# First block's pooled up, up and output projections as three split products

## The chip, the cores and the metric

The kernel runs on one core of one Trainium2 chip. The metric is the device time in microseconds (us) of one execution. A core has five engines with queues of their own: PE (TensorE, matrix products), DVE (VectorE), ACT (ScalarE), POOL (GpSimd) and SP (SyncE, which here issues the loads). Semaphores order their work. SBUF is the on-chip memory, PSUM the banks into which PE writes.

## What is computed

Two transformer-like blocks, one after the other, on 256 tokens of width 1024, all in float32. The first block, where the change lies:

```python
ada = c @ w_ada[layer] + b_ada[layer]
shift1, scale1, gate1, shift2, scale2, gate2 = split(ada, 6)
h = rms_norm(x, g_norm1) * (1.0 + scale1) + shift1
z = h @ w_in
zq, zk, zv, ziq, zik, ziw, zp, zg = split(z, cuts)
...
y_attn = dsa_attention(q, k, zv, iq, ik, ziw) @ w_up_attn[layer]   # 512 -> 1024
y_pool = pool_mixer(zp, w_pool_grp, s_pool) @ w_up_pool[layer]     # 512 -> 1024
g_attn, g_pool = split(sigmoid(zg), 2)
mixed = (g_attn * y_attn + g_pool * y_pool) @ w_out[layer]         # 1024 -> 1024
x = x + gate1 * mixed
h2 = rms_norm(x, g_norm2) * (1.0 + scale2) + shift2
x = x + gate2 * peer_ffn(h2, w_peer_q, peer_subkeys, peer_u, peer_v)
```

`dsa_attention` has 8 heads of 64 and lets each token see 64 chosen positions; `peer_ffn` is dense here over all 128 x 128 experts. The second block (recurrent branch, sparse attention, feed-forward) comes after it and isn't touched beyond the naming of two buffers.

## The kernel before

**The stream of weights.** All weight matrices lie in one stream of quarters of 128 x 1024 numbers (512 KB). `ORDER` (from `plan`) is the order of the blocks: ada0 to ada3, in0 to in6, up_pool, ada9, ada4, up_attn, out0, out1, pq0, pq1, the expert matrices u and v, then the second block. A block is four quarters. Blocks in `PAIRED` alternate with an ada block, quarter by quarter: in1 with ada6, in6 with ada7, up_pool with ada8, out0 with ada5, out1 with ada10, pq1 with ada11. SP loads quarter b into slot b % 4 of `ring`, strictly in the order of the stream; it waits until `left[b % 4]` says that quarter b - 4 has left its slot. A quarter that isn't free holds up all loads behind it.

**Two kinds of quarters.** A quarter marked in `SPLIT` is taken apart: ACT rounds it into `high` (`round_quarter`), POOL subtracts to give `low` (`lower_quarter`) and thereby frees the ring slot; PE makes a product as three (`product`, high x high, high x low, low x high), and its end (`multiplied`) frees the slot of `high` and `low`. The moving or stationary input is kept as a pair too (`hTh`, `hTl`). Any other quarter is read straight from the ring: PE's product is then one full-precision matmul (the profile shows two records of it), and the ring slot is free when PE is done. The ada quarters are read by DVE, two `scalar_tensor_tensor` of 128x512 each (the first one a `tensor_scalar`), which add up `c @ w_ada` by rows; PE sums over the partitions later (`ada`). Before the change `in`, `pq`, `u`, `v` and the second block's weights are split; up_pool, up_attn, out0 and out1 are not. `high` and `low` have four slots, chosen by b % 4 like the ring's, so in a paired block only two of them are used.

**Order by hand.** Each engine runs its own program from top to bottom. ACT's roundings stand where the program calls `ahead(name, q, n)`: it rounds every split quarter up to n quarters behind quarter q of that block; `wait_product` calls it with n = 3 and then waits for PE. A rounding that has to wait for its load or its slot holds up all that ACT has to do behind it.

**The stretch of the change,** in PE's order: `z1(6)` (in6), up_pool (`token_major`, 4 quarters of 4 products 128x512, 2 token tiles by 2 halves), the attention of 8 units (`attention("a1")`: logits, transposes, values, in a software pipeline with ACT's Exp and copies and DVE's maxima, normalizations and copies; DVE also adds up ada9 and ada4, one quarter a unit), up_attn (its last two quarters output by output, `bank_done`), the transposes of the gated mix M1 (`transposes("m1")`), the sums of ada6 to ada9, out0, the first half of out1 (`out1(0, 1)`), the sums of ada4 and ada5 which give gate1, the second half of out1 (`out1(2, 3)`, both quarters waited for before its first product), the second norm and pq0.
DVE, behind the attention: the pooled branch times its gate (L1648), some constants of the second block (L1650 to L1662, 22 short steps), the gating of the four outputs of up_attn (L1671, L1672), half of the copies of M1's transposes, ada5, ada10, then x1 from out0 and out1 (L1694, L1695).
ACT, behind the attention: the two halves of its output (L1155), half of M1's copies (`keep_turned`, L1030), the copies of the gate (L1162), the squares of x1 (L998).

## Time and profile before

| | us |
|---|---|
| median of 3 runs | 1657.17 |
| lowest, highest | 1652.24, 1659.6 |
| the profiled execution | 1656.26 |
| its span in the trace | 1654.4 |
| PE busy in the span | 1556.4 |
| DVE, ACT, POOL busy | 1101.6, 840.4, 1103.9 |
| mean granted clock of PE | 0.977 |

Times in the trace count from the start of the span. The clock is a share of 2.4 GHz and has two levels, 1.0 and 0.5; a mean between them tells how much of the stretch ran at each. The profile's busy times of PE are those of its matmuls; weight loads (PEld) run beside them.

### The profile page before, as it was taken

The numbers are of one execution on the slowest core, as the hardware profiler recorded it, in microseconds if no ns is written. First come the engines' busy times: TensorE is split into PE (matmuls) and PEld (weight loads), VectorE is DVE, ScalarE is ACT, GpSimd is POOL, SyncE is SP. The second block draws the span as 40 slices with busy tenths as digits, with TensorE's granted clock in tenths as the row PEclk, the third lists the DMA queues.
The fourth block names the chain that finished last, engine by engine and source line by source line (L and its number), as shares of the span: only waits on it lengthen the run. The fifth ranks groups of instructions, "written<-read, shape, count | busy, mean of one in ns | idle before, by whom it ended". The sixth has DMA issues, their size and how long they took to land. (4 is left out here: it accounts for less than half of the span.)

```text
span 1654.4 us, 27016 instructions
## 1 busy us (share of the span) xinstructions
PE 1556.4 (94%) x9679; PEld 1359.3 (82%) x9679; DVE 1101.6 (67%) x1666; ACT 840.4 (51%) x1437; POOL 1103.9 (67%) x453
## 2 busy tenths in 40 slices
PE   2898898999999999999999999999999988999999
PEld 2685537999999999988888888888888756799987
DVE  5563645999937777768888888761756275368850
ACT  1454215555566666655445554547764354554443
POOL 0771006889986666658888888855985621688896
PEclk9999789999999999999999999999999889999999
DMA  7665355455454444435555555545554510455554
GB/s 278 207 230 203 127 181 201 165 178 178 153 190 141 140 141 141 141 127 190 190 194 193 196 190 191 198 141 176 192 192 140 166 52 26 153 179 182 187 179 140
DMA packets 77397, 280.07 MB, mean 169 GB/s; under 512 B 8577, under 2 KB 9089, under 8 KB 77186
## 3 DMA queue, kind: packets, MB, share of 16 engines
q1 hardware_dynamic: 76592, 276.68, 49.3%
q10 hardware_dynamic: 722, 2.27, 0.4%
q8 instruction: 55, 0.90, 0.2%
q14 instruction: 28, 0.23, 0.1%
HBM read 277.86 MB, written 1.05 MB: 169 GB/s over the span
## 5 line engine op out<-in xcount | busy, mean ns | idle before, releaser
L2071 POOL TENSOR_TENSOR low<-ring,high 128x1024 fp32r<-128x1024 f32 x449 | 1103.7, 2470 | 539.9 <-ACT high L977 539.3
L977 ACT ACTIVATE high<-ring 128x1024 fp32r<-128x1024 f32 x449 | 472.8, 1058 | 438.1 <-PE PS L346 381.7
L344 PE MATMUL PS<-hTh,high 128*128 128x256 f32 (+1 forms) x1648 | 472.7, 287 | 9.7 <-POOL low L2071 7.5
L346 PE MATMUL PS<-hTh,low 128*128 128x256 f32 (+1 forms) x1648 | 467.9, 284 | 0.0
L345 PE MATMUL PS<-hTl,high 128*128 128x256 f32 (+1 forms) x1648 | 467.8, 284 | 0.0
L344 PE MATMUL PS<-high,hTh 128*128 128x512 f32 x940 | 370.6, 394 | 14.4 <-POOL low L2071 5.9
L345 PE MATMUL PS<-low,hTh 128*128 128x512 f32 x940 | 367.9, 391 | 0.0
L346 PE MATMUL PS<-high,hTl 128*128 128x512 f32 x940 | 367.8, 391 | 0.0
L1801 DVE TENSOR_TENSOR hTl<-region,hTh 128x256 fp32r<-128x256 f32 x128 | 289.2, 2261 | 57.9 <-ACT hTh L1231 57.9
L344 PEld LDWEIGHTS PS<-hTh,high 128*128 128x128 f32 (+1 forms) x1648 | 316.3, 192 | 13.0 <-POOL low L2071 9.2
L345 PEld LDWEIGHTS PS<-hTl,high 128*128 128x128 f32 (+1 forms) x1648 | 316.2, 192 | 0.0
L346 PEld LDWEIGHTS PS<-hTh,low 128*128 128x128 f32 (+1 forms) x1648 | 315.8, 192 | 0.0
L344 PEld LDWEIGHTS PS<-high,hTh 128*128 128x128 f32 x940 | 177.9, 189 | 54.4 <-issue 10.4
L346 PEld LDWEIGHTS PS<-high,hTl 128*128 128x128 f32 x940 | 177.7, 189 | 37.3
L345 PEld LDWEIGHTS PS<-low,hTh 128*128 128x128 f32 x940 | 178.1, 189 | 36.4
L1204 ACT ACTIVATE onehot<-gate,gate_rest 128x128 fp32r<-128x128 f32 x256 | 82.1, 391 | 66.8 <-DVE gate L1763 66.8
L1560 DVE SCALAR_TENSOR_TENSOR region<-ring,cols,region 128x512 f32<-128x512 f32 x84 | 75.3, 897 | 49.6 <-DMA ring<-in_stream 46.5
L1774 DVE TENSOR_TENSOR region<-region,PS 128x256 f32<-128x256 f32 (+31 forms) x64 | 35.3, 551 | 61.6 <-PE PS L771 61.6
L342 PE MATMUL PS<-ring,region 128*128 128x512 f32 x128 | 63.5, 654 | 3.0 <-ACT region L1083 1.2
L771 PE MATMUL PS<-onehot 128*128 128x128 f32 x256 | 60.7, 276 | 0.0
L342 PEld LDWEIGHTS PS<-ring,region 128*128 128x128 f32 x128 | 26.1, 210 | 38.8 <-issue 31.5
L770 PE MATMUL PS<-onehot 128*128 128x128 f32 x256 | 57.1, 261 | 0.7 <-ACT onehot L1204 0.7
(283 smaller groups left out, 1535.1 us busy)
## 6 DMA issues: line engine op xcount, KB each, us to landing
ring<-in_stream SPq DMA_DIRECT2D x523, 512.0 KB, 3.3
X<-in_x SPq DMA_DIRECT2D x1, 1024.0 KB, 5.1
region<-in_band ACTq DMA_DIRECT2D x1, 1024.0 KB
result<-X SPq DMA_DIRECT2D x4, 256.0 KB, 2.0
region<-in_skeys ACTq DMA_DIRECT2D x1, 512.0 KB
region<-in_consts ACTq DMA_DIRECT2D x1, 352.0 KB, 3.4
region<-in_wpool ACTq DMA_DIRECT2D x1, 256.0 KB
cols<-in_cols SPq DMA_DIRECT2D x1, 208.0 KB, 5.1
```

The source lines that it names most:

```text
L342: return pe.matmul(out_, stat, mov, start=start, stop=stop, **kw)
L344: pe.matmul(out_, sh, mh, start=start, stop=False, **kw)
L345: pe.matmul(out_, sh, ml, start=False, stop=False, **kw)
L346: return pe.matmul(out_, sl, mh, start=False, stop=stop, **kw)
L770: pe.matmul(dst, rows[:, j, :], high_[:, j, :], start=True, stop=False)
L771: last = pe.matmul(dst, rows[:, j, :], rest[:, j, :], start=False, stop=True)
L977: act.activation(high[:, b % RING, :], ring[:, b % RING, :], ACT.Copy).then_inc(rounded[b % RING], 1)
L1204: ins = act.activation(fours(onehot[:, 2, g % 2, :])[:, j, :], fours(second[:, g % 2, :])[:, j, :], ACT.Copy, scale=gate_rest[:, 4 * g + j ...
L1560: ins = dve.scalar_tensor_tensor(ada_acc(j), w[:, c, :], col("cT", 2 * q + c), ada_acc(j), ALU.mult, ALU.add)
L1774: dve.tensor_tensor(v[:, 0:n, :], v[:, 0:n, :], placed[:, 0:n, :], ALU.mult)
L1801: dve.tensor_tensor(lo, src, hi.bitcast(F32), ALU.subtract).then_inc(sem("weights_split"), 1)
L2071: pool.tensor_tensor(low[:, b % RING, :], ring[:, b % RING, :], high[:, b % RING, :].bitcast(F32), ALU.subtract).then_inc(left[b % RING], 1)
```

## The change

The quarters of up_pool, up_attn, out0 and out1 are split as well. The slot in `high` and `low` (and of `rounded` and `multiplied`) is no longer b % 4 but the number of split quarters before b, modulo 4 (`part`); the ring and `left` stay at b % 4. The pooled input becomes a pair (`pool_parts`: ACT rounds, POOL subtracts, in POOL's order just before up_pool's first quarter). The attention's output goes as a pair into the first half of hT (DVE subtracts, behind the attention and ahead of L1648), and the transposed mix as a pair into hT (`mixed_high`, `mixed_low`) in place of `keep_turned`. ACT's roundings of the new quarters are placed: up_pool's first with `z1(6)`, its second behind the copies of in6, its last two behind the two sigmoids; up_attn's, one each, at the end of the last four steps of the attention; out0's first two behind the attention's output, its third behind `mixed_high`, its fourth and out1's first two behind the copy of the ada sums, out1's last two behind the two copies of gate1. The diff, cut:

```diff
--- before.py
+++ after.py
@@ -121,13 +121,21 @@
-SPLIT = [NAME_AT[b].rstrip("0123456789") in ("in", "pq", "u", "v", "rx", "ry", "z", "ro", "ao", "oo", "fg", "fv",
+SPLIT = [NAME_AT[b].rstrip("0123456789") in ("in", "up_pool", "up_attn", "out", "pq", "u", "v", "rx", "ry", "z", "ro", "ao", "oo", "fg", "fv",
                                                 "dn") for b in range(N_QUARTERS)]
...
+SPLIT_NO = [0] + np.cumsum(SPLIT).tolist()
+
+
+def part(b):
+
+    return SPLIT_NO[b] % RING
+
+
 def nth_split(b):
-    return sum(SPLIT[i] for i in range(b % RING, b + 1, RING))
+    return SPLIT_NO[b] // RING + 1
@@ -217,10 +225,10 @@
         poolT = take(4, S)
-        OT1 = take(4, S)
+        pool_parts = Pair(onehot[:, w, :, :].rearrange("p a n -> p (a n)") for w in (1, 2))
         late_acc = take(ADA_B - 4, NB)
         y_pool = XN1
-        M1, MT1 = N1, NT1
+        M1 = N1
         LB1 = band.rearrange("p t g s -> p (t g s)")[:, 0:3 * 2 * S].rearrange("p (u e k) -> p u e k", u=3, e=2)
@@ -322,7 +330,7 @@
             if SPLIT[b]:
-                eng.wait_ge(multiplied[b % RING], nth_split(b))
+                eng.wait_ge(multiplied[part(b)], nth_split(b))
             else:
...
@@ -347,13 +355,14 @@
+        MIXED1, MIXED2 = 0, KC // 2
         TURNS = ("n1", "m1", "n2", "n3", "q2", "c2", "k2", "pz", "m2", "n4")
...
-        KEPT = {"m1": KC, "q2": KC, "k2": KC, "c2": 2 * KC, "pz": KC}
+        KEPT = {"q2": KC, "k2": KC, "c2": 2 * KC, "pz": KC}
@@ -404,7 +413,10 @@
             b = quarter_no(name, q)
-            ins.then_inc((multiplied if SPLIT[b] else left)[b % RING], 1)
+            if SPLIT[b]:
+                ins.then_inc(multiplied[part(b)], 1)
+            else:
+                ins.then_inc(left[b % RING], 1)
@@ -521,15 +533,15 @@
             def token_major(name, src, bank, per=2, rows=P, first=True, last=True, inner=NB, c0=0, norm=None,
-                            bank_done=None, quarters=range(QUARTERS), mixed=False):
+                            bank_done=None, quarters=range(QUARTERS), mixed=None):
...
                         pe.wait_ge(sem("norm_split"), nth_norm(norm, KC // 2, (per * h + per + 1) // 2))
-                    if mixed:
-                        pe.wait_ge(sem("mixed_split"), h + 1)
+                    if mixed is not None:
+                        pe.wait_ge(sem("mixed_split"), mixed + h + 1)
                     w = slot(name, h, inner)
@@ -691,23 +703,23 @@
             pe.wait_ge(sem("z_kept"), 2 * Z1B)
-            token_major("up_pool", poolT, lambda t, o: 4 + (2 + 2 * t + o) % 4, per=1, inner=D)
+            pe.wait_ge(sem("pool_split"), 1)
+            token_major("up_pool", pool_parts.rearrange_all(S), lambda t, o: 4 + (2 + 2 * t + o) % 4, per=1, inner=D)
             pe.wait_ge(sem("y_pool_kept"), 4)
...
-            pe.wait_ge(sem("attn1_kept"), 2)
-            token_major("up_attn", OT1, lambda t, o: 4 + 2 * t + o, per=1, inner=D, bank_done="up_done")
+            pe.wait_ge(sem("attn1_split"), 2)
+            token_major("up_attn", hT, lambda t, o: 4 + 2 * t + o, per=1, inner=D, bank_done="up_done")
             transposes("m1", M1, "m1_ready", 4, first_half=3)
...
                 ada(j)
-            pe.wait_ge(sem("turned_kept"), kept_by("m1", KC))
             def out1(*quarters, done=None):
-                token_major("out1", MT1, lambda t, o: 5 + 2 * t, quarters=quarters, bank_done=done)
-
-            token_major("out0", MT1, lambda t, o: 4 + 2 * t)
+                token_major("out1", hT, lambda t, o: 5 + 2 * t, quarters=quarters, bank_done=done)
+
+            token_major("out0", hT, lambda t, o: 4 + 2 * t, mixed=MIXED1)
             pe.wait_ge(sem("ada_kept"), 2)
...
@@ -936,7 +948,7 @@
             for half in range(2):
-                token_major(f"oo{half}", hT, lambda t, o, half=half: 4 + 2 * t + half, mixed=(half == 0),
+                token_major(f"oo{half}", hT, lambda t, o, half=half: 4 + 2 * t + half, mixed=None if half else MIXED2,
                             bank_done="oo_done" if half else None)
@@ -973,9 +985,9 @@
                 if nth_split(b) > 1:
-                    act.wait_ge(multiplied[b % RING], nth_split(b) - 1 + r)
-                act.activation(high[:, b % RING, :], ring[:, b % RING, :],
-                               ACT.Copy).then_inc(rounded[b % RING], 1)
+                    act.wait_ge(multiplied[part(b)], nth_split(b) - 1 + r)
+                act.activation(high[:, part(b), :], ring[:, b % RING, :],
+                               ACT.Copy).then_inc(rounded[part(b)], 1)
@@ -1018,6 +1030,13 @@
+            def mixed_high(tag):
+
+                for c in range(0, KC, 2):
+                    act.wait_ge(sem("turned"), turned_by(tag, c // 2 + 1))
+                    act.activation(hTh[:, c:c + 2, :], PS[:, c // 2, :].rearrange("p (c s) -> p c s", c=2),
+                                   ACT.Copy).then_inc(sem("mixed_rounded"), 1)
+
             def keep_turned(tag, dst, scale=None, shift=None):
@@ -1060,6 +1079,8 @@
                         kept(u - 2)
+                    if tag == "a1" and u >= n - 2:
+                        ahead("up_attn", u - (n - 2), 0)
                     if tag == "a2" and u == n // 2 + 2:
@@ -1137,12 +1158,16 @@
                                scale=col("gain1", 0)).then_inc(sem("qk1_kept"), 1)
+            act.wait_ge(sem("pool_kept"), 4)
+            act.activation(tuple(pool_parts)[0], poolT.rearrange("p g s -> p (g s)"),
+                           ACT.Copy).then_inc(sem("pool_rounded"), 1)
             z1(6)
+            ahead("up_pool", 1, 0)
             act.wait_ge(sem("z_kept"), 2 * Z1B)
...
                                ACT.Sigmoid).then_inc(sem("sig1"), 1)
-            wait_used(act, "up_pool")
+            wait_product("up_pool")
             for t in range(T):
@@ -1152,15 +1177,19 @@
                 act.wait_ge(sem("a1_values"), (t + 1) * H1 // 2)
-                act.activation(OT1[:, :, t * P:(t + 1) * P], PS[:, 6 + t, :].rearrange("p (c q) -> p c q", c=4),
-                               ACT.Copy).then_inc(sem("attn1_kept"), 1)
-            keep_turned("m1", MT1)
+                act.activation(hTh[:, 0:4, t * P:(t + 1) * P], PS[:, 6 + t, :].rearrange("p (c q) -> p c q", c=4),
+                               ACT.Copy).then_inc(sem("attn1_rounded"), 1)
+            ahead("out0", 1, 0)
+            mixed_high("m1")
+            ahead("out0", 2, 0)
             act.wait_ge(sem("ada_summed"), 8)
             act.activation(adaT[:, 24:40], PS[:, 7, 24:40], ACT.Copy).then_inc(sem("ada_copied"), 1)
+            ahead("out1", 1, 0)
             for i in range(2):
...
                                ACT.Copy).then_inc(sem("gate1_kept"), 1)
+            ahead("out1", 3, 0)
             sumsq("n2", XN1, "x1_ready")
...
@@ -1378,10 +1407,7 @@
                     ahead(f"ao{half}", q)
-            for c in range(0, KC, 2):
-                act.wait_ge(sem("turned"), turned_by("m2", c // 2 + 1))
-                act.activation(hTh[:, c:c + 2, :], PS[:, c // 2, :].rearrange("p (c s) -> p c s", c=2),
-                               ACT.Copy).then_inc(sem("mixed_rounded"), 1)
+            mixed_high("m2")
             for half in range(2):
@@ -1459,6 +1485,13 @@
                     ins.then_inc(sem("norm_split"), 1)
+
+            def mixed_low(done):
+
+                for c in range(0, KC, 2):
+                    dve.wait_ge(sem("mixed_rounded"), done + c // 2 + 1)
+                    dve.tensor_tensor(hTl[:, c:c + 2, :], PS[:, c // 2, :].rearrange("p (c s) -> p c s", c=2),
+                                      hTh[:, c:c + 2, :].bitcast(F32), ALU.subtract).then_inc(sem("mixed_split"), 1)
@@ -1641,6 +1674,11 @@
             attention("a1")
+            for t in range(T):
+                qs = slice(t * P, (t + 1) * P)
+                dve.wait_ge(sem("attn1_rounded"), t + 1)
+                dve.tensor_tensor(hTl[:, 0:4, qs], PS[:, 6 + t, :].rearrange("p (c q) -> p c q", c=4),
+                                  hTh[:, 0:4, qs].bitcast(F32), ALU.subtract).then_inc(sem("attn1_split"), 1)
@@ -1671,7 +1709,7 @@
                                       ALU.add).then_inc(sem("m1_ready"), 1)
-            keep_turned("m1", MT1)
+            mixed_low(MIXED1)
@@ -2004,10 +2042,7 @@
                                       ALU.add).then_inc(sem("m2_ready"), 1)
-            for c in range(0, KC, 2):
-                dve.wait_ge(sem("mixed_rounded"), c // 2 + 1)
-                dve.tensor_tensor(hTl[:, c:c + 2, :], PS[:, c // 2, :].rearrange("p (c s) -> p c s", c=2),
-                                  hTh[:, c:c + 2, :].bitcast(F32), ALU.subtract).then_inc(sem("mixed_split"), 1)
+            mixed_low(MIXED2)
             for half in range(2):
@@ -2067,12 +2102,17 @@
-                pool.wait_ge(rounded[b % RING], nth_split(b) + r)
-                pool.tensor_tensor(low[:, b % RING, :], ring[:, b % RING, :], high[:, b % RING, :].bitcast(F32),
+                pool.wait_ge(rounded[part(b)], nth_split(b) + r)
+                pool.tensor_tensor(low[:, part(b), :], ring[:, b % RING, :], high[:, part(b), :].bitcast(F32),
                                    ALU.subtract).then_inc(left[b % RING], 1)
...
             for b in range(START["in0"], first):
+                if b == quarter_no("up_pool", 0):
+                    high_, low_ = tuple(pool_parts)
+                    pool.wait_ge(sem("pool_rounded"), 1)
+                    pool.tensor_tensor(low_, poolT.rearrange("p g s -> p (g s)"), high_.bitcast(F32),
+                                       ALU.subtract).then_inc(sem("pool_split"), 1)
                 if SPLIT[b]:
```

## Rows read from the trace of the kernel before

**Rows 1.** The page, section 1: busy us, share of the span, instructions by engine.

```profile
PE 1556.4 (94%) x9679; PEld 1359.3 (82%) x9679; DVE 1101.6 (67%) x1666; ACT 840.4 (51%) x1437; POOL 1103.9 (67%) x453
```

**Rows 2.** Windows by stage; the header names the columns.

```profile
core 0: us, PE busy (x) PEld busy (x) DVE busy (x) ACT busy (x) POOL busy (x), PEclk, DMA share, GB/s
...
139.80:157.40 17.60, 14.27 (x32) 5.88 (x32) 4.60 (x7) 8.16 (x10) 0.00 (x0) 1.00 0.59 217
157.40:184.40 27.00, 22.24 (x120) 14.26 (x120) 24.04 (x50) 11.88 (x44) 0.00 (x0) 0.64 0.55 187
184.40:200.40 16.00, 15.96 (x33) 6.85 (x34) 8.29 (x29) 0.00 (x0) 0.00 (x0) 0.87 0.20 66
...
207.10:231.90 24.80, 23.76 (x48) 9.77 (x49) 8.84 (x14) 0.18 (x1) 0.00 (x0) 0.89 0.58 209
231.90:236.50 4.60, 4.60 (x11) 1.28 (x9) 1.50 (x2) 0.60 (x1) 0.00 (x0) 1.00 0.64 232
236.50:245.30 8.80, 8.80 (x17) 3.59 (x16) 5.49 (x8) 4.25 (x9) 0.00 (x0) 0.81 0.08 17
245.30:257.00 11.70, 5.99 (x30) 5.38 (x30) 9.68 (x18) 6.14 (x11) 2.35 (x1) 0.71 0.61 216
```

**Rows 3.** Timeline of weight loads: split products (in6), then full-precision ones (up_pool).

```profile
128.62 0.19 PEld L344 LDWEIGHTS PS<-high,hTh 128*128 128x128 f32 x1
...
129.30 0.19 PEld L344 LDWEIGHTS PS<-high,hTh 128*128 128x128 f32 x1
...
142.35 0.19 PEld L342 LDWEIGHTS PS<-ring,region 128*128 128x128 f32 x1 [0.24 <-issue]
142.78 0.19 PEld L342 LDWEIGHTS PS<-ring,region 128*128 128x128 f32 x1 [0.24 <-issue]
```

**Rows 4.** Groups by form, 120 to 262 us (count, busy, mean ns); DMA issues (landing us).

```profile
L1560 DVE SCALAR_TENSOR_TENSOR region<-ring,cols,region 128x512 f32<-128x512 f32 x41 | 30.8, 751 | 33.2 <-DMA ring<-in_stream 32.2
L2071 POOL TENSOR_TENSOR low<-ring,high 128x1024 fp32r<-128x1024 f32 x6 | 14.2, 2377 | 129.8 <-ACT high L977 129.8
...
L977 ACT ACTIVATE high<-ring 128x1024 fp32r<-128x1024 f32 x8 | 8.1, 1048 | 6.7 <-PE PS L346 6.7
...
ring<-in_stream SPq DMA_DIRECT2D x47, 512.0 KB, 3.3
```

**Rows 5.** Timeline (start us, us, engine), POOL and DVE where their work overlaps.

```profile
63.02 2.77 DVE L1560 SCALAR_TENSOR_TENSOR region<-ring,cols,region 128x512 f32<-128x512 f32 x1 [1.28 <-DMA ring<-in_stream]
...
65.42 2.62 POOL L2071 TENSOR_TENSOR low<-ring,high 128x1024 fp32r<-128x1024 f32 x1 [0.18 <-ACT high L977]
...
250.71 2.35 POOL L2071 TENSOR_TENSOR low<-ring,high 128x1024 fp32r<-128x1024 f32 x1 [113.99 <-ACT high L977]
...
251.63 1.97 DVE L1456 TENSOR_TENSOR hTl<-region,hTh 128x512 fp32r<-128x512 f32 x1
```

**Rows 6.** Timeline, end of the attention: ACT's copies, DVE's normalization and ada4.

```profile
174.66 0.38 ACT L1055 ACTIVATE region<-PS 128x256 f32<-128x256 f32 x1
...
176.99 0.69 DVE L1508 TENSOR_TENSOR region<-region 128x512 f32<-128x512 f32 x1
...
177.84 0.38 ACT L1055 ACTIVATE region<-PS 128x256 f32<-128x256 f32 x1
...
177.94 1.53 DVE L1560 SCALAR_TENSOR_TENSOR region<-ring,cols,region 128x512 f32<-128x512 f32 x2
```

**Rows 7.** Timeline, DVE behind the attention: pooled branch, chain's end, last gating.

```profile
182.21 2.47 DVE L1648 TENSOR_TENSOR region<-region 128x1024 f32<-128x1024 f32 x2
...
189.10 0.17 DVE L1662 TENSOR_SCALAR sp<-sp 126x11 f32<-126x11 f32 x1
...
201.31 0.69 DVE L1672 TENSOR_TENSOR region<-PS,region 128x512 f32<-128x512 f32 x1
```

**Rows 8.** Timeline: second gate copy, DVE on out1's last output, the norm's transposes.

```profile
236.59 0.60 ACT L1162 ACTIVATE region<-PS 128x512 f32<-128x512 f32 x1 [1.51 <-PE PS L509]
...
245.34 0.70 DVE L1694 TENSOR_TENSOR PS<-PS,region 128x512 f32<-128x512 f32 x1 [2.01 <-PE PS L342]
...
249.12 2.74 PE L483 MATMUL PS<-ident,region 128*128 128x128 f32 x16 [3.82 <-ACT region L1006]
```

More of the change, by code:

```diff
@@ L744, in peer_u @@
                                    hT[:, c, :], start=(c == 0), stop=(c == KC - 1))
-                last.then_inc(multiplied[b % RING], 1)
+                last.then_inc(multiplied[part(b)], 1)
             pe.wait_ge(sem("scores_kept"), 8)
@@ L790, in peer_v @@
                                        skip_group_check=True)
-                last.then_inc(multiplied[b % RING], 1)
+                last.then_inc(multiplied[part(b)], 1)
             pe.wait_ge(sem("ada_kept"), 4)
@@ L816, in _ @@
                         if t and half:
-                            last.then_inc(multiplied[b % RING], 1)
+                            last.then_inc(multiplied[part(b)], 1)
                     if not (t and half):
```

6 lines of the change are left out of this document (3 added, 3 removed).

## The prediction

> **What bounds the kernel now.** I read the page first. PE is busy for 94% of the span, DVE and POOL for 67% each [rows 1], and from the expert products on the matmuls of one stage follow those of the next without a gap. So whatever the first block's projections shift, everything behind them is shifted by as much. I then cut the stretch of the change into its stages [rows 2]: the pooled up projection (139.8 to 157.4 us), the attention (157.4 to 184.4), the attention's up projection (184.4 to 200.4), `out0` with the first half of `out1` (207.1 to 231.9), the two gate sums (231.9 to 236.5), the second half of `out1` (236.5 to 245.3), and the second norm. PE is busy for nearly all of each projection stage: they are bound by the full-precision products. In none of them does POOL do anything. That last column matters most below. The mean granted clock of a stage tells how long PE ran at the lower of its two levels (1.2 GHz against 2.4): 0.87 over 16.0 us is 2 x 0.13 x 16.0 = 4.2 us at half, 0.89 over 24.8 us is 5.5 us, 0.81 over 8.8 us is 3.3 us.
>
> **What is removed.** A full-precision product shows as two records. Their weight loads stand 0.43 us apart at 2.4 GHz [rows 3], so one costs 0.86 us. A split product shows as three; equal loads stand 0.68 us apart for 512 columns at 2.4 GHz [rows 3]. 0.43 us is the time of two passes of 512 columns at 2.4 GHz; at 1.2 GHz a pass takes 0.43, so the products cost 1.71 and 1.28. The change makes 4 quarters x 4 = 16 products in each of up_pool, up_attn, out0 and out1, 64 in all: 64 x 0.174 = 11.1 us of PE at full clock, and 0.43 instead of 0.17 each at half clock.
>
> The Trainium skill ("FP8 and Floating Point Precision", TensorE Precision Notes) says that true FP32 makes four passes through the array; three of four would save 25%, 13.7 us over the 64 products. The pitches give 20%, and the sum goes by them.
>
> **What is added.** Each of the 16 quarters now gets a rounding on ACT (1.05 us) and a subtraction on POOL (2.38 us), one after the other [rows 4]. The ring slot is given back when POOL is done, 3.4 us after the rounding starts; before, it was given back after PE's four products, also 3.4 us. The load behind it still needs 3.3 us to land [rows 4]. New too: one rounding and one subtraction for the pooled input (`pool_parts`), DVE subtractions for the attention output and the mixed input (0.7 us each for 128x512), and larger copies on ACT in place of `keep_turned`.
>
> **The price that isn't in the instruction counts** is DVE against POOL. When POOL starts a subtraction at 250.71 and DVE, at 251.63, a `tensor_tensor` whose inputs both lie in SBUF, DVE's ends at 253.60, 0.54 us after POOL's (253.06). At 63.02 a DVE `scalar_tensor_tensor` beside another subtraction takes 2.77 us; POOL's next, asked for at 65.42 while that one finishes (65.79), takes 2.62 itself [rows 5]. The same DVE instruction takes 0.75 us where POOL is idle [rows 4]. So the two exclude each other for whole instructions, first come first served: a DVE instruction with two SBUF inputs that meets a subtraction waits up to 2.4 us.
>
> The Trainium skill ("SBUF — State Buffer", Who interferes with whom) states this: a DVE instruction with two SBUF inputs contends with a GpSimd instruction that reads SBUF, and the later one blocks fully. By that rule the trace agrees; the rule speaks against this change, which puts POOL work where POOL has now been idle for 114 us.
>
> **The sum, stage by stage,** on the profiled execution's own clock. I replay each queue in its program order with the durations above.
>
> *in6 and up_pool: 0.* The rotation over split quarters lets in6's third quarter be rounded without waiting for its first one's products: some 0.5 us. up_pool's quarters 2 and 3 are rounded only behind the sigmoids, so PE waits some 3 us (146.2 to 149.5) before quarter 2. Sixteen products at 0.68 with that wait end near 155.3, where the 16 full-precision ones end now. Everything in the stage (two ACT roundings, `pool_parts`, DVE's ada8) is then paid for.
>
> *Attention: +7.2.* The four up_attn quarters are rounded in ACT's last four steps. The first is rounded when ACT is free at 175.04 [rows 6], its subtraction runs 176.1 to 178.5. DVE's unit-6 normalization, now at 176.99 [rows 6], waits and ends at 179.0. The next rounding runs from 178.2 (after the copy of 177.84 [rows 6]), so the second subtraction holds 179.3 to 181.7; DVE's last two accumulations for ada4, now 177.94 to 179.47 [rows 6], meet it and the third one (182.2 to 184.5) and end at 185.05 instead. Up_attn's last quarter is loaded behind them: issued 185.1, landed 188.4, rounded 189.5. In the meantime unit 7's normalization runs at 185.4, 5.8 us late, and its values end at 188.6. ACT copies the two output halves behind that rounding (190.7), DVE subtracts the second (191.6). PE starts up_attn at 191.6 instead of 184.44. Of this 5.6 us are waits for POOL; without them it would be +1.5.
>
> *up_attn: +0.1.* With 4.3 us at half clock first, 3.4 products are made, the other 12.6 take 8.6 us; the first output would be ready at 200.5. But DVE's gating of the pooled branch and the decay chain, now 182.21 to 189.3 [rows 7], begin at 191.6 and meet the subtractions for out0's first two quarters (197.6 to 202.7): they end at 203.4. The four outputs take DVE 4 x 1.46 us, to 209.3, now 202.0 [rows 7]. The transposes and ada sums behind (PE, 5.1 us from 202.0 to out0's start at 207.1) are unchanged, and hide the split of the mixed input. out0 starts at 214.4 instead of 207.1: +7.3.
>
> *out0, out1: -0.5.* out0's fourth quarter is behind a quarter of ada5 in SP's queue, whose slot DVE frees at 216.4; it lands at 220.3, is rounded, and lowered at 224.4. By then PE, after 5.5 us at half clock, is at 225.2: no wait. out1's first quarters are lowered at 227.2 and 231.2, PE is done with them at 233.9. 24 products took 19.5 us, now 24.8. The gate sums end at 238.4 (4.5 us), ACT copies the second gate (0.6 us [rows 8]), and only then rounds out1's last two quarters: 239.0, two roundings, then 2 x 2.38 us on POOL. PE needs both and starts at 244.9: **6.5 us idle**, the new wait. Now the same chain costs nothing, as the quarters lie in the ring. Eight products then take 5.5 us, or 7.2 if the first 3.4 us run at half clock. I take 7.2: the pause of 3.8 us before the norm's transposes (245.3 to 249.12 [rows 8]) is followed today by a clock of 0.71 in that stage [rows 2]. The last x1 is at 253.6; now at 245.34 + 1.42 = 246.8 [rows 8]. Together +6.8.
>
> *After that: 0.* pq0's first rounding and the norm are chains of ACT and DVE as before. pq1's quarters rotate better, but the last one's rounding stands behind a copy that waits for PE either way.
>
> The sum is 1656.26 + 6.8 = **1663 us**. The profiled execution lies 0.9 us below the median of 1657.17; the three runs spread over 7 us. Against the median this is +0.35%. About 0.5%, 8.3 us, is what a measurement here can tell from no change, so this is *no change, on the slower side*.
>
> Not shown by the trace, with bounds. A DVE instruction on the decay chain is 126x11: whether it too is excluded is between 0 and 4.5 us (two subtractions met); its nearest rows are the 128x512 ones, so I take it as excluded. Two-input normalization in the attention: 0 to 5.6 us, taken in full for the same reason. ACT's rounding between two Exp: 0 to 1.3 us for a table load; the copies there today bring none, so 0. The pause of up_pool: 0 to 1.7 us for clock, taken as 0, as 3.3 us lies under the 3.8 after which it fell; it may go either way.
>
> **Rivals.**
> A, *the exclusion doesn't reach these instructions.* For it: they are smaller than those in rows 5, and POOL runs few. Against: rows 5, both forms. The waits of 5.6 in the attention and of 3 us on the decay chain vanish; up_attn starts at 186.0, out0 at 206.0, the pause before out1's last quarters stays, x1 ends at 243 to 244.6. That is -2.2 to -3.9: 1653. Chance 0.13.
> B, *slower by over 0.5%: one more stretch at half clock.* PE's pauses grow (3.3 us in up_pool, a longer attention tail, 6.5 us before out1). Every further 3.4 us at half clock costs 1.7 us, and the time passes 1665.5, 0.5% over the median, with 2.4 us on top of my sum: from two such stretches on (3.4), or from one with one more subtraction met by DVE (1.7 + 1.9). Both stretches and the subtraction give 1663.1 + 5.3 = 1668. For it: the attention stage is already at 0.64 [rows 2]. Against: pauses also let loads and roundings run ahead. Chance 0.33.
> C, *faster by over 0.5%.* The 11.1 us of PE reach the end: neither the exclusion nor the 6.5 us pause is there, because ACT and POOL are ahead wherever they are needed. A's -3 and the pause's -6.5: 1647. Against it is ACT's program order, in which the two roundings stand behind the gate copies. Chance 0.07.
> D, *the rotation does nothing or more than the 0.5 us of in6.* In the stages with all quarters split the buffers are the same as now. The paired stretches in1 and pq1 wait for loads or for an ACT order that stays. It would be 1662 or 1664, inside the forecast.
>
> **How the numbers follow.** Forecast 0.47 (1659 to 1665.4; D lies in it), A 0.13, B 0.33, C 0.07. Within 0.5%: 0.47 + 0.13 = 0.60; slower 0.33; faster 0.07. For 8 in 10 the range takes in A and most of B: 1652 to 1670, leaving out C and B's end.
>
> **What the profile after would show.** PE products of the four projections as three records 0.68 apart. DVE normalizations of units 6 and 7, and the last ada4 accumulations, at 1.9 to 2.8 us. up_attn starting some 7 us later against in6's end; PE idle for about 6 us, released by POOL, between the gate sums and out1's end. If POOL's subtractions run beside DVE instructions of 0.7 us, the attention term is wrong; if PE has no wait there, the out1 term is. Wrong altogether if up_pool's quarters are late by more than 3 us, or if DVE picks up the attention later than the replay.

## The result, and the profile after

The changed kernel takes 1664.49 us (median of 11 runs, 1662.13 to 1668.36), the kernel before in the same comparison 1653.80 us (11 runs, 1646.96 to 1660.14): ratio 1.007, interval 1.0051 to 1.0089. It is slower by 10.7 us. The predicted time of 1663 us is 1.5 us off and the range holds it; but the predicted *difference*, 0.35%, is half of the measured one, and 0.7% is past the 0.5% up to which the forecast spoke of no change. By the ratio this is rival B, given 0.33; by the time it isn't, as B begins at 1665.5 us and 1664.49 lies within the forecast's 1659 to 1665.4. The two disagree because the three runs of before that were shown (median 1657.17) lie 3.4 us over all eleven. The profiled execution took 1662.13 us, its span 1660.3.

Section 1 of the page of the changed kernel answers [rows 1]:

```profile
PE 1546.7 (93%) x9743; PEld 1375.3 (83%) x9743; DVE 1125.1 (68%) x1668; ACT 858.0 (52%) x1454; POOL 1144.4 (69%) x470
```

PE is busy for 9.7 us less, near the 11.1 us of the split products, and the kernel is longer all the same. The windows of the changed kernel, by stage, answer [rows 2]: in6 from its ninth TensorE record on (1.9 us behind its first) with up_pool; attention; up_attn; transposes and ada sums; out0 with half of out1; gate sums; second half of out1 up to the norm's transposes. Then the same stages of the *kernel before in a second execution*, profiled later (e12 below):

```profile
core 0: us, PE busy (x) PEld busy (x) DVE busy (x) ACT busy (x) POOL busy (x), PEclk, DMA share, GB/s
127.80:157.60 29.80, 22.97 (x89) 17.14 (x87) 12.84 (x10) 14.61 (x17) 16.14 (x7) 0.94 0.59 212
157.60:191.40 33.80, 22.07 (x121) 14.10 (x121) 28.76 (x51) 15.51 (x48) 9.36 (x4) 0.63 0.47 160
191.40:205.20 13.80, 13.69 (x48) 10.77 (x48) 12.86 (x31) 2.12 (x2) 5.33 (x3) 0.80 0.29 103
205.20:211.50 6.30, 5.99 (x48) 5.75 (x49) 3.89 (x6) 3.11 (x5) 2.10 (x1) 0.92 0.00 0
211.50:232.10 20.60, 19.79 (x73) 15.43 (x74) 13.19 (x15) 3.37 (x4) 7.51 (x4) 0.86 0.72 254
232.10:242.70 10.60, 4.18 (x9) 1.07 (x7) 5.32 (x8) 5.79 (x10) 4.65 (x2) 0.77 0.26 93
242.70:254.70 12.00, 8.18 (x24) 6.28 (x24) 3.84 (x8) 2.48 (x7) 0.00 (x0) 0.78 0.36 140
```

```profile
128.20:156.30 28.10, 23.87 (x73) 12.98 (x71) 6.93 (x11) 10.27 (x11) 4.76 (x2) 1.00 0.54 195
156.30:183.20 26.90, 21.41 (x121) 13.63 (x121) 24.10 (x50) 11.78 (x44) 0.00 (x0) 0.68 0.56 187
183.20:197.00 13.80, 13.80 (x32) 6.00 (x33) 8.24 (x29) 0.00 (x0) 0.00 (x0) 1.00 0.23 76
197.00:203.10 6.10, 5.47 (x49) 5.24 (x49) 2.81 (x6) 1.21 (x4) 0.00 (x0) 1.00 0.48 173
203.10:227.80 24.70, 23.12 (x50) 9.56 (x50) 8.85 (x14) 0.18 (x1) 0.00 (x0) 0.93 0.57 199
227.80:231.90 4.10, 4.10 (x9) 1.07 (x7) 1.43 (x2) 0.60 (x1) 0.00 (x0) 1.00 0.82 288
231.90:242.90 11.00, 7.19 (x18) 3.00 (x17) 7.99 (x15) 6.08 (x14) 0.00 (x0) 1.00 0.46 164
```

Three things stand in these lines. POOL's column is no longer empty behind the attention's start. PE is idle for 11.7 us of the attention (before 5.5) and for 6.4 us of the gate sums' window (before 0). And the granted clock is under 1 in all seven stages of the changed kernel, in two of the second execution of before.

The table lays out every kernel of this study in that way. A column is the time from the first TensorE record of one part (for in6 the ninth) to that of the next in the profiled execution, in brackets the us of it at 1.2 GHz, 2 x (1 - granted clock) x length.

| kernel | in6, up_pool | attention | up_attn | sums | out0, half of out1 | gate sums | rest of out1 | all |
|---|---|---|---|---|---|---|---|---|
| before | 28.1 (0) | 27.0 (20) | 15.9 (4.3) | 6.8 (1.4) | 25.2 (5.5) | 4.1 (0) | 12.6 (3.4) | 119.8 |
| e12, before again | 28.2 (0) | 26.8 (17) | 13.8 (0) | 6.1 (0) | 24.7 (3.4) | 4.1 (0) | 11.0 (0) | 114.7 |
| after | 29.8 (3.4) | 33.8 (25) | 13.9 (5.5) | 6.3 (1.0) | 20.6 (5.8) | 10.6 (4.9) | 12.0 (5.3) | 127.0 |
| e11, after again | 28.4 (0) | 33.8 (26) | 15.9 (4.4) | 5.9 (0.3) | 20.7 (3.1) | 10.6 (4.4) | 12.3 (5.8) | 127.7 |
| e1, lowering late | 29.9 (3.4) | 28.2 (17) | 18.7 (5.1) | 10.2 (10) | 20.9 (5.3) | 10.6 (5.7) | 11.6 (4.8) | 130.1 |
| e2, rounding early | 29.9 (3.4) | 33.9 (25) | 14.1 (5.9) | 6.1 (0.7) | 20.8 (6.1) | 5.8 (0) | 11.1 (4.3) | 121.7 |
| e3, both | 30.1 (3.4) | 28.3 (20) | 18.9 (5.2) | 10.2 (10) | 20.5 (5.9) | 5.3 (0) | 11.1 (3.7) | 124.3 |
| e4, rotation alone | 26.8 (0) | 26.9 (17) | 13.8 (0) | 6.4 (0.6) | 24.1 (2.9) | 4.1 (0) | 11.0 (0) | 113.0 |
| e5, POOL alone | 28.6 (0) | 32.2 (21) | 13.8 (0) | 6.1 (0) | 23.9 (3.4) | 4.1 (0) | 11.0 (1.2) | 119.7 |
| e6, POOL writes | 28.1 (0) | 26.7 (16) | 16.2 (4.8) | 6.5 (0.8) | 25.6 (6.0) | 4.1 (0) | 12.7 (3.4) | 119.9 |
| e7, up_attn whole | 30.1 (3.4) | 26.9 (18) | 16.6 (5.5) | 6.2 (0.2) | 25.6 (10) | 4.1 (0) | 9.6 (0) | 118.9 |
| e8, out0 and out1 | 26.9 (0) | 26.9 (18) | 16.6 (5.6) | 6.2 (0.1) | 25.5 (10) | 4.4 (0) | 9.7 (0) | 116.1 |
| e9, out1 alone | 27.0 (0) | 26.9 (17) | 13.8 (0) | 6.1 (0) | 26.9 (6.8) | 5.1 (0) | 9.5 (0.5) | 115.3 |
| e10, no rotation | 30.5 (3.4) | 33.8 (26) | 13.7 (4.4) | 7.0 (2.6) | 31.2 (15) | 10.6 (3.4) | 11.1 (4.3) | 137.9 |

Read it by columns: a stage's length is a matter of PE's passes, its pauses and its time at 1.2 GHz, and the last differs between two executions of one kernel (up_attn of before: 4.3 us at half once, none in the other, 2.1 us apart). "Half clock" below is the 1.2 GHz of the brackets.

### The profile page after: what moved, and what is told of

It is laid out like the page before. It is cut to its first block and busy times, and to the rows that moved or that the text cites. A ratio compares the mean times of both kernels' runs of the same rounds, so it can differ in the third digit from the quotient of the medians.

```text
span 1660.3 us, 27119 instructions
## 1 busy us (share of the span) xinstructions
PE 1546.7 (93%) x9743; PEld 1375.3 (83%) x9743; DVE 1125.1 (68%) x1668; ACT 858.0 (52%) x1454; POOL 1144.4 (69%) x470
## 5 line engine op out<-in xcount | busy, mean ns | idle before, releaser
L2106 POOL TENSOR_TENSOR low<-ring,high 128x1024 fp32r<-128x1024 f32 x465 | 1142.2, 2469 | 505.3 <-ACT high L989 504.7
L989 ACT ACTIVATE high<-ring 128x1024 fp32r<-128x1024 f32 x465 | 489.5, 1057 | 452.4 <-PE PS L354 376.3
L352 PE MATMUL PS<-high,hTh 128*128 128x512 f32 x988 | 392.9, 398 | 21.9 <-POOL low L2106 11.3
L353 PE MATMUL PS<-low,hTh 128*128 128x512 f32 x988 | 389.9, 395 | 0.0
L354 PE MATMUL PS<-high,hTl 128*128 128x512 f32 x988 | 389.5, 394 | 0.0
L352 PEld LDWEIGHTS PS<-hTh,high 128*128 128x128 f32 (+1 forms) x1648 | 316.2, 192 | 12.7 <-POOL low L2106 8.5
L352 PEld LDWEIGHTS PS<-high,hTh 128*128 128x128 f32 x988 | 189.1, 191 | 65.0 <-issue 19.2
L354 PEld LDWEIGHTS PS<-high,hTl 128*128 128x128 f32 x988 | 188.7, 191 | 40.3
L1593 DVE SCALAR_TENSOR_TENSOR region<-ring,cols,region 128x512 f32<-128x512 f32 x84 | 89.0, 1059 | 28.9 <-DMA ring<-in_stream 25.9
L495 PE MATMUL PS<-ident,region 128*128 128x128 f32 x160 | 27.6, 343 | 31.3 <-ACT region L1018 23.5
L495 PEld LDWEIGHTS PS<-ident,region 128*128 128x128 f32 x160 | 24.6, 179 | 34.6 <-issue 15.5
```

Source lines behind the costliest of these rows:

```text
L352: pe.matmul(out_, sh, mh, start=start, stop=False, **kw)
L353: pe.matmul(out_, sh, ml, start=False, stop=False, **kw)
L354: return pe.matmul(out_, sl, mh, start=False, stop=stop, **kw)
L495: last = pe.transpose(PS[:, c // 2, (c % 2) * S + t * P:(c % 2) * S + (t + 1) * P], src[:, t, c * P:(c + 1) * P], ident[:, :])
L989: act.activation(high[:, part(b), :], ring[:, b % RING, :], ACT.Copy).then_inc(rounded[part(b)], 1)
L1593: ins = dve.scalar_tensor_tensor(ada_acc(j), w[:, c, :], col("cT", 2 * q + c), ada_acc(j), ALU.mult, ALU.add)
```

## The experiments

**The attention (e5, e6).** Does POOL's subtraction make the attention late, or ACT's new work and the late load? Both kernels are the one before with the same ACT copies, and three POOL instructions behind them:

```diff
 ACT, in attention("a1")
+                    if tag == "a1" and n - 2 <= u < n + 1:
+                        act.activation(high[:, (0, 1, 3)[u - (n - 2)], :], high[:, 2, :].bitcast(F32),
+                                       ACT.Copy).then_inc(sem("extra_rounded"), 1)
 ACT, ahead of out1's further roundings
+            act.wait_ge(sem("extra_done"), 3)
 POOL, ahead of up_attn's quarters
+                    for k in range(3):
+                        pool.wait_ge(sem("extra_rounded"), k + 1)
+                        pool.tensor_tensor(low[:, (0, 1, 3)[k], :], low[:, 2, :].bitcast(F32),
+                                           high[:, (0, 1, 3)[k], :].bitcast(F32), ALU.subtract).then_inc(sem("extra_done"), 1)
+                    pool.wait_ge(sem("extra_done"), 3)
 POOL in e6, in place of the subtraction
+                        pool.memset(low[:, (0, 1, 3)[k], :].bitcast(F32), 0.0).then_inc(sem("extra_done"), 1)
```

> The kernel before, with three ACT copies and three POOL subtractions of 128x1024 put into the end of the attention, where the changed kernel has those of up_attn's first three quarters; their results are used by nobody. All projections stay full precision. Theory (DVE instructions with two SBUF inputs wait for POOL's subtraction): unit 6's normalization takes 1.9 to 2.1 us instead of 0.69, ada4's last two accumulations 4.5 to 5.6 us instead of 1.53, and the attention's up projection starts 5 to 6 us later than in the kernel before (some 190 instead of 184.4 us, counted from the same start of the attention). Rival (the attention's tail is late because of ACT's roundings between the Exp, or the late load): DVE's instructions keep 0.69 and 1.53 us and the projection starts at most 1.5 us later.

> As the run with POOL's subtractions alone, but POOL fills the same three 128x1024 tiles with zeros (it writes SBUF and reads nothing). If what excludes DVE is that POOL reads SBUF, DVE's normalization and accumulations keep 0.69 and 1.53 us and up_attn starts within 1.5 us of the kernel before. If any POOL instruction on SBUF excludes them, they stretch as beside the subtractions, by the length of the fill, and up_attn starts later by 2 us or more.

Timelines (start us, us, engine, line, operation) of e5, then of e6: DVE's normalization (L1512; of unit 6 in e5, of unit 7 in e6) and ada4's last accumulations (L1564) beside POOL:

```profile
174.97 2.43 POOL L2083 TENSOR_TENSOR low<-low,high 128x1024 fp32r<-128x1024 f32 x1 [39.09 <-ACT high L1064]
175.90 2.05 DVE L1512 TENSOR_TENSOR region<-region 128x512 f32<-128x512 f32 x1
178.15 5.10 POOL L2083 TENSOR_TENSOR low<-low,high 128x1024 fp32r<-128x1024 f32 x2 [0.75 <-ACT high L1064]
178.21 5.59 DVE L1564 SCALAR_TENSOR_TENSOR region<-ring,cols,region 128x512 f32<-128x512 f32 x2
```

```profile
177.39 1.53 DVE L1564 SCALAR_TENSOR_TENSOR region<-ring,cols,region 128x512 f32<-128x512 f32 x2
178.68 0.95 POOL L2083 MEMSET low<- 128x1024 f32 x1 [2.23 <-ACT high L1064]
179.03 0.69 DVE L1512 TENSOR_TENSOR region<-region 128x512 f32<-128x512 f32 x1
```

The two take 2.05 and 5.59 us beside the subtractions, 0.69 and 1.53 beside the fill (unit 6's normalization in e6, at 176.45, begins as the first fill ends and tells nothing). The fills are shorter, 0.95 us against 2.43, and lie beside DVE's instructions for 0.6 and 0.2 us only; but neither DVE nor POOL waits there. The attention takes 32.16 us in e5 and 26.74 in e6, no more than in the kernel before. The two kernels share ACT's copies, so the 5.4 us are POOL's alone, and come where it reads SBUF. Their whole times (1653.36 and 1660.83 us, one execution each) go the other way: e6 has 15 us at half clock between the attention and the norm, e5 has 5, and one execution can't size 5 us of 1650. What DVE does beside the two kinds of POOL's work is the rule of the Trainium skill ("SBUF — State Buffer", Who interferes with whom): a GpSimd instruction that only writes does not contend with a DVE instruction of two SBUF inputs. The trace agrees.

**Moving the wait away (e1).** POOL begins up_attn's subtractions only behind the last normalization:

```diff
+                if b == quarter_no("up_attn", 0):
+                    pool.wait_ge(sem("a1_norm"), H1)
```

> The kernel after with one more wait: POOL begins up_attn's four subtractions only when DVE has made the attention's last normalization. ACT's roundings stay. My theory (POOL and DVE exclude each other, 5.6 us of the attention's tail is DVE waiting): unit 6's normalization is back at 0.69 us from 2.04, the last two accumulations of ada4 at 1.5 from 5.59, up_attn starts 5 to 6 us earlier against the attention's start; DVE's pooled branch now meets subtractions (up to 2.4 us more), up_attn's last quarters come late by 2 to 3 us; net 2 to 4 us faster than the kernel after. Rival (the rounding on ACT in the chain is the price, POOL isn't): no more than 1 us comes back.

1666.13 us (6 runs), ratio 1.0071 (1.0052 to 1.009): nothing gained. The attention did get shorter by 5.6 us, but the subtractions now meet the next DVE work:

```profile
182.88 7.99 POOL L2106 TENSOR_TENSOR low<-ring,high 128x1024 fp32r<-128x1024 f32 x3
185.99 5.96 DVE L1686 TENSOR_TENSOR region<-region 128x1024 f32<-128x1024 f32 x2
192.24 4.83 POOL L2106 TENSOR_TENSOR low<-ring,high 128x1024 fp32r<-128x1024 f32 x2 [1.38 <-ACT high L989]
192.45 2.23 DVE L1690 TENSOR_TENSOR sp<-sp 126x11 f32<-126x11 f32 x1
194.71 2.39 DVE L1691 TENSOR_TENSOR sp<-sp 126x11 f32<-126x11 f32 x1
200.72 0.69 DVE L1709 TENSOR_TENSOR PS<-PS,region 128x512 f32<-128x512 f32 x1
```

The pooled branch takes 5.96 us (2.47 where POOL is idle [rows 7]), two links of the decay chain 2.23 and 2.39 (0.17 each). The gating starts at 200.72; in the changed kernel's first execution at 201.05. DVE's chain from the attention to the gating is what up_attn's outputs wait for, and it pays for the subtractions wherever they are put. The transposes behind then ran at half clock throughout (10.2 us).

**The pause before out1's last quarters (e2, e3).**

```diff
-            ahead("out1", 1, 0)
+            ahead("out1", 3, 0)
             for i in range(2):
...
-            ahead("out1", 3, 0)
```

> The kernel after with out1's last two roundings moved ahead of the two copies of gate1 on ACT. Theory (the 6.46 us in which PE is idle before out1's last quarters are ACT's order, not the loads): the quarters are loaded by 229.4 and 232.7, rounded by 233.8, lowered by 236.2, the idle time falls to under 1 us, and the products that ran at half clock behind it run at full, 1.7 us more: 6 to 8 us faster than the kernel after. Rival (the loads or POOL set it): 0 to 2 us.

> Both edits. Theory: the two costs are in series, so the gains add: 8 to 12 us faster than the kernel after, that is from 2 us slower to 4 us faster than the kernel before by its profiled execution's sum. Rival (the extra time is the granted clock, whatever the pauses): the gains don't add, and it stays over 0.5% slower than before.

e2: 1661.19 us (12 runs), ratio 1.0037 (1.0021 to 1.0053), 0.33% or 5.5 us under the changed kernel's, though the two intervals just touch; the stretch of the table is 5.3 us shorter. The wait of PE, in the changed kernel and in e2:

```profile
242.74 0.77 PE L352 MATMUL PS<-high,hTh 128*128 128x512 f32 x1 [6.46 <-POOL low L2106]
```

```profile
240.49 0.77 PE L352 MATMUL PS<-high,hTh 128*128 128x512 f32 x1 [1.67 <-POOL low L2105]
```

4.8 us of pause are gone and about 5.5 gained: this wait was on the path in full, and about half of the loss. e3, with e1's edit on top: 1662.22, 1.004 (1.0019 to 1.0062), the same as e2; e1's edit is worth nothing here either.

**Which projections pay (e7, e8, e9).** e7 is e2 with up_attn in full precision; e8 leaves up_pool in full precision too; e9 splits out1 alone, with e2's order of roundings, and makes the pair of the mixed input later, on ACT and DVE from the copy that out0 reads. Where a projection isn't split, the work for its pair of inputs goes with it. The line of SPLIT:

```diff
 e7: ... in ("in", "up_pool", "out", "pq", ...)
 e8: ... in ("in", "out", "pq", ...)
 e9: ... in ("in", "pq", ...) or NAME_AT[b] == "out1"
```

> The changed kernel with out1's quarters rounded before the gate copies, and with up_attn left in full precision, so that POOL has nothing to do in the attention, nor beside the decay chain. Theory (the loss is POOL against DVE around the attention): the attention takes 27 us as in the kernel before, up_attn starts at its time, out0 begins where it did (some 50 us after the attention's start) and the two output projections save up to 5.5 us of PE. Median 4 to 6 us below the kernel before (ratio 0.997), so 10 us below the run with the early roundings alone. Rival (three-record products lose by themselves, through PE's clock or the loads, wherever they are): ratio 1.001 to 1.004, above the kernel before still.

> As the run with up_attn whole, but up_pool in full precision too: only the two output projections are split. Theory (up_pool's gain of 2.7 us on PE is paid for by the pause before its third quarter and by ACT's two more roundings): within 1.5 us of that run. If up_pool's split is worth its PE time, this one is 2 to 3 us slower; if its pause costs more, through the clock too, 2 us or more faster.

> The kernel before with the rotation over split quarters and out1 alone split (mixed input rounded and lowered from the kept copy, out1's quarters rounded before the gate copies); up_pool, up_attn and out0 in full precision. Theory (a split gains only where its quarters lie loaded early enough to hide 3.4 us of rounding and lowering): the 16 products of out1 save 2.8 us, the second half of out1 takes 9.6 us as in the two runs with it split early instead of 11.0, and the ratio to the kernel before is 0.997 (rotation alone 0.9985, and 2.8 us less). Rival (the new subtractions delay ada5 and ada10 on DVE and through them out1's loads): PE waits 2 us or more for POOL ahead of out1's first quarters, and the ratio is 0.999 or above.

| | products split | PE us saved at full clock (x 0.174) | median, us | ratio to before |
|---|---|---|---|---|
| e7 | 48 | 8.4 | 1657.68 | 1.0029 (1.0008 to 1.0051) |
| e8 | 32 | 5.6 | 1654.94 | 1.0002 (0.9981 to 1.0022) |
| e9 | 16 | 2.8 | 1655.90 | 1.0013 (0.9998 to 1.0028) |

Here my theory fell, as far as it went for the whole loss. The attention is back at 26.9 us in all three, and the second half of out1 takes 9.5 to 9.7 us instead of 11.0 (8 x 0.174 = 1.4, as priced); yet none of the three is measurably faster than the kernel before. e9 shows why at its plainest, around out1's first quarter:

```profile
217.63 1.06 ACT L991 ACTIVATE high<-ring 128x1024 fp32r<-128x1024 f32 x1 [13.43 <-DMA ring<-in_stream]
218.77 2.63 POOL L2101 TENSOR_TENSOR low<-ring,high 128x1024 fp32r<-128x1024 f32 x1 [85.39 <-ACT high L991]
221.54 0.47 PE L353 MATMUL PS<-high,hTh 128*128 128x512 f32 x1 [3.88 <-POOL low L2101]
```

The quarter lands at 217.63, which is 62.7 us behind the attention's start, as in e4 below (62.8): the load isn't late. PE, free at 217.66, could take it at once in full precision; it waits 3.88 us for the rounding and the subtraction: more than 16 products save. In e8 PE waits for out0's fourth quarter in the same stage:

```profile
207.35 2.37 POOL L2094 TENSOR_TENSOR low<-ring,high 128x1024 fp32r<-128x1024 f32 x1 [1.69 <-ACT high L989]
207.38 2.38 DVE L1704 TENSOR_TENSOR adaT<-adaT,cols 128x16 f32<-128x16 f32 x1 [1.16 <-ACT adaT L1180]
...
216.37 1.06 ACT L989 ACTIVATE high<-ring 128x1024 fp32r<-128x1024 f32 x1 [9.02 <-DMA ring<-in_stream]
217.50 2.34 POOL L2094 TENSOR_TENSOR low<-ring,high 128x1024 fp32r<-128x1024 f32 x1 [7.78 <-ACT high L989]
...
219.89 0.80 PE L353 MATMUL PS<-high,hTh 128*128 128x512 f32 x1 [4.36 <-POOL low L2094]
```

A DVE instruction on 128x16 elements meets a subtraction and takes 2.38 us; ada5 and the ring slots that it frees are later by that. The quarter lands at 216.37, 0.8 us after PE is free, and 3.5 us of rounding and lowering come on top. From the stage's first product to the landing it is 10.8 us, no longer than in full precision (11.9 in e4, where PE doesn't wait for it): PE with split products is there sooner, and the quarter has to be ready 3.5 us before that. PE pauses for 4.36 us, and 10 us of the stage run at half clock against 3.4 and 5.5 in the two executions of before.

e7 has the same pause, and it shows where the time went that the attention gave back:

```profile
224.07 0.80 PE L353 MATMUL PS<-high,hTh 128*128 128x512 f32 x1 [4.74 <-POOL low L2099]
```

out0's fourth quarter lands 61.4 us behind the attention's start in e2 and 60.8 in e7, but PE begins out0 54.1 us behind it in e2 and 49.6 in e7. The stage takes 20.8 us there and 25.6 here. POOL's delay in the attention had hidden the wait for this quarter; without it the wait is PE's.

e7 against e8 is the price of up_pool's split: 30.1 against 26.9 us in the first column (28.4 in e11, which has no half clock there), 0.27% by the medians' ratios, though the intervals overlap. The pause before its third quarter (3.08 us at 150.22 in e7, 2.87 in the changed kernel) is followed by 3.4 us at half clock in six of the seven executions that have this split, and in none of the seven without it is there any in that column.

**The rotation (e4, e10).** e4 is the kernel before with `part(b)` and `nth_split(b)` as in the change and nothing else; e10 is the changed kernel with these two lines back:

```diff
-    return SPLIT_NO[b] % RING
+    return b % RING
-    return SPLIT_NO[b] // RING + 1
+    return sum(SPLIT[i] for i in range(b % RING, b + 1, RING))
```

> The kernel before with nothing but the rotation of the split buffers over split quarters. Theory: in6 ends 0.5 us earlier, all else as before: -0.5 us, not to be told from before (ratio 0.998 to 1.002). Rival (the rotation is worth something in the paired blocks in1, in6 and pq1): 2 us or more faster.

> The changed kernel with the split buffers numbered by the ring slot, as in the kernel before, so that a split projection paired with a full precision one has two of the four buffers. Theory (the loss has nothing to do with the buffers, and the rotation gave the 1.3 us by which the stretch from in5 to the attention got shorter with the rotation alone): 1 to 3 us slower than the changed kernel, ratio to the kernel before 1.008 to 1.009. Rival (the rotation costs something in the changed kernel, as roundings run further ahead and POOL meets DVE more often): faster than the changed kernel, ratio 1.005 or less.

e4: 1652.26 us (12 runs), ratio 0.9985 (0.9967 to 1.0003); in6 and up_pool take 26.8 instead of 28.1 us. e10: 1676.11 (4 runs), 1.0133 (1.011 to 1.0156). In the changed kernel the rotation is worth 0.63%, 10.4 us; without it the change would have cost 22. e10's timeline of ACT, POOL and PE in the out0 stage:

```profile
218.94 1.06 ACT L989 ACTIVATE high<-ring 128x1024 fp32r<-128x1024 f32 x1 [8.94 <-PE PS L354]
219.91 0.16 ACT L1186 ACTIVATE adaT<-PS 128x16 f32<-128x16 f32 x1
...
229.16 1.06 ACT L989 ACTIVATE high<-ring 128x1024 fp32r<-128x1024 f32 x1 [9.09 <-DMA ring<-in_stream]
230.29 2.34 POOL L2106 TENSOR_TENSOR low<-ring,high 128x1024 fp32r<-128x1024 f32 x1 [7.84 <-ACT high L989]
...
232.69 0.79 PE L352 MATMUL PS<-high,hTh 128*128 128x512 f32 x1 [7.16 <-POOL low L2106]
```

With two buffers for out0's quarters, the rounding of the third waits for PE's products with the first (8.94 us). Behind it in ACT's program stands the copy of `adaT`: 219.91 instead of 211.70 in the changed kernel. DVE's ada5 starts behind that copy, the slots come free late, the fourth quarter lands at 229.16 instead of 218.76 (the stage itself began 2.4 us later), and PE pauses for 7.16 us, with 15 us of the stage at half clock.

**Second executions (e11, e12)**, both kernels unchanged:

> The changed kernel once more, for a second profiled execution. If the stage times of the first are the kernel's own, the attention takes 33 to 34.5 us, up_pool with in5 and in6 29.5 to 30.5 us and the gate sums with the pause 10 to 11 us again; if they are chance of PE's clock, one of them moves by 2 us or more.

> The kernel before once more, for a second profiled execution. If its first one was a slow draw of PE's clock in up_attn (4.3 us at half), this execution has less at half clock in up_attn and out1, and a time of 1645 to 1653 us; if not, it has the same stretches and 1654 to 1658 us.

e11 (1662.75 us) repeats the attention and the gate sums to 0.1 us; in6 and up_pool are 1.4 us shorter, with no time at half clock, and up_attn is 2.0 longer. That isn't the clock (4.4 us at half against 5.5), but DVE's decay chain, which here meets both subtractions for out0's first quarters; PE waits for the gating behind it:

```profile
196.65 4.84 POOL L2106 TENSOR_TENSOR low<-ring,high 128x1024 fp32r<-128x1024 f32 x2 [6.01 <-ACT high L989]
196.78 2.29 DVE L1697 TENSOR_SCALAR sp<-sp 126x11 f32<-126x11 f32 x1
199.11 2.40 DVE L1698 TENSOR_SCALAR sp<-sp 126x11 f32<-126x11 f32 x1
205.97 1.09 PE L495 MATMUL PS<-ident,region 128*128 128x128 f32 x8 [2.68 <-DVE region L1710]
```

e12 took 1648.33 us: no half clock in up_attn and out1's end, and 5.1 us less in the whole stretch than the execution on which the prediction was built.

## Why the prediction went as it did

*The sum, against the execution that it was made on.* +6.8 us were predicted, the stretch from in6 to the norm is 127.0 - 119.8 = 7.2 us longer. By stages:

| step | predicted | measured |
|---|---|---|
| in6 and up_pool | 0 | +1.7 (e11: +0.3) |
| attention | +7.2 | +6.7 |
| up_attn and the sums | +0.1 | -2.5 |
| out0, out1, gate sums | -0.5 | +1.2 |

*Attention: right, and by the cause named.* The stage is 6.7 us longer (7.2 predicted). That up_attn also begins at 191.36 us, where 191.6 was predicted, is luck in part: in6 began 1.5 us sooner than in the execution of before (125.83 against 127.37, in e12 126.22), and up_pool took that back. The normalization takes 2.04 us and the accumulations 5.59; e5 and e6 tie it to POOL's reads. Rival A falls with it.

*up_attn: the chain was excluded, by one subtraction in the first execution and by two in the second.* This is the step that the trace of before couldn't show, and the bound of 4.5 us was taken in full. The first execution:

```profile
198.36 4.93 POOL L2106 TENSOR_TENSOR low<-ring,high 128x1024 fp32r<-128x1024 f32 x2 [6.44 <-ACT high L989]
198.47 2.32 DVE L1699 TENSOR_TENSOR sp<-sp 126x11 f32<-126x11 f32 x1
200.83 0.17 DVE L1700 TENSOR_SCALAR sp<-sp 126x11 f32<-126x11 f32 x1
201.05 0.70 DVE L1709 TENSOR_TENSOR PS<-PS,region 128x512 f32<-128x512 f32 x1
```

The link at 198.47 takes 2.32 us in place of 0.17, so 126x11 elements are enough. But the subtractions began 0.8 us later than in the replay, when the chain was nearly at its end: its last instruction, at 200.83, began before the second subtraction (200.89) and kept its 0.17 us. Gating began at 201.05 (203.4 predicted), 2.4 us sooner. In e11 (lines above) both were met, 2.29 and 2.40 us, and the gating began 11.8 us behind up_attn's first product, as predicted. So the term was right in kind, and whether it is paid once or twice differs between two executions.

*out0 and out1: the pause was right (6.46 us, 6.5 predicted), the products around it were not quite.* out0 with half of out1 took 20.6 us where 19.5 were predicted. Of the 1.1 us, the waits for out1's first quarters (0.58 and 0.23 us, in the replay one of about 0.5) and the clock (5.8 us at half, 5.5 assumed) make up to 0.5; the rest no single wait explains. The last products took 7.9 instead of 7.2, with 5.3 us at half where 3.4 were taken.

*in6 and up_pool: a term set to nothing.* The pause was predicted at 3.3 us and is 2.87; its half clock was bounded by 0 and 1.7 us and taken as 0. It came in six of seven executions. And the rotation's 0.5 us were 1.3, so that the split itself costs 3.2 (e7 against e8; 1.5 by e11, without half clock), not the 0.5 that were to cancel.

*The base: part of why the difference came out at half.* The two profiled executions differ by 5.9 us (1662.13 - 1656.26), where 6.8 were predicted; the medians differ by 10.7. The execution of before lies 2.5 us over the median of its eleven, that of the changed kernel is the fastest of its eleven, 2.4 us under their median. For the first part there is a reason on record: the half clock in up_attn (4.3 us) and out1 (3.4) was read from one execution of before [rows 2] as a property of the kernel, and the second one has neither and is 5.1 us shorter in the stretch. The changed kernel has 51 and 44 us at half there, before 34 and 21. So the prediction compared with a before that was long by the very thing that the change brings on. That is rival B's mechanism, pauses that bring more time at half clock; I priced it on top of the sum instead of in it. The second part stays open: both profiled executions of the changed kernel (1662.13 and 1662.75) lie under its median, and no trace shows what the slower ones do.

*The time of 1663 us is luck in part.* It rests on a median of before that is 3.4 us too high and a difference that is 4.8 us too small (5.9 for 10.7), and the two errors cancel to 1.5.

*Rival C* had its pause removed by e2 and the exclusion removed by e7 and e8, and still there was no gain: 11.1 us of PE don't reach the end because the quarters of out0 and of out1's first half come just in time, and the split lays 3.5 to 3.9 us between landing and use (e8, e9). *Rival D* gave the rotation 0.5 us where it is worth 10.4: only the rounding that it frees was looked at, not what stands behind that rounding in ACT's program, the copy of `adaT`.

*Open.* Why PE's clock falls behind a pause in one execution and not in the next, no row decides, nor why the decay chain meets one subtraction or two. Whether earlier loads (a longer ring) would hide rounding and lowering wasn't tried. No kernel of the study is measurably faster than before; the rotation alone, 0.9985 with 1 inside its interval, is nearest.

## What to carry to other kernels

A cheaper product that needs a prepared operand pays only where the operand has landed long before PE wants it: ask of each load how long it lies before its use, not only what PE saves. Work given to POOL must be placed against DVE's instructions with two SBUF inputs and its TENSOR_SCALARs on SBUF, however small they are, and moving it off one instruction of a dependent chain onto the next gains nothing (e1); moving it past the whole chain wasn't tried. And take PE's clock in a stage from two executions before you build a difference of half a per cent on it.

## What the runs showed of the hardware

A DVE instruction of 126x11 or 128x16 elements, 0.17 us by itself, takes 2.2 to 2.4 us when it meets POOL's subtraction: in the changed kernel, e1 and e8 a TENSOR_TENSOR with both inputs in SBUF, in e11 a TENSOR_SCALAR of 126x11 (2.29 and 2.40 us). And e8's timeline has a larger TENSOR_SCALAR whose one tensor input is in SBUF:

```profile
209.99 0.49 DVE L1584 TENSOR_SCALAR region<-ring,cols 128x512 f32<-128x512 f32 x1
...
220.54 2.85 POOL L2094 TENSOR_TENSOR low<-ring,high 128x1024 fp32r<-128x1024 f32 x1 [0.70 <-ACT high L989]
221.09 2.60 DVE L1584 TENSOR_SCALAR region<-ring,cols 128x512 f32<-128x512 f32 x1
```

0.49 us with POOL idle, 2.60 beside a subtraction, so a single tensor input is no protection; the gating, whose first operand is in PSUM, kept its 0.70 us in the changed kernel beside the subtraction that ended at 203.29. The Trainium skill ("SBUF — State Buffer", Who interferes with whom) counts tensor_scalar among the instructions that may take the ports shared with GpSimd; by that rule, the trace agrees.
